# Group norm in the trips of the RWKV scan, the first norm joined to the parameter block, key tile 0 among the low-rank products

## What is computed

```python
u = rms_norm(h, norm1_g[i])
xs = h[:, :, None, :] + (prev - h)[:, :, None, :] * mu        # h here is u, prev is u one token earlier
rkv = jnp.einsum('btjd,jde->btje', xs[:, :, :3], w_in)         # r, k, v
decay, a, gate = ...                                           # low-rank products: w1 w2, a1 a2, g1 g2
def step(S, inp):                                              # S: 64 x 64 for each head
    sa = jnp.einsum('bhvk,bhk->bhv', S, -kk_t)
    S = S * w_t[:, :, None, :] + sa[..., None] * (kk_t * a_t)[:, :, None, :] + v_t[..., None] * k_t[:, :, None, :]
    return S, jnp.einsum('bhvk,bhk->bhv', S, r_t)
mean = jnp.mean(y, axis=-1, keepdims=True)                     # group norm: over the 64 of each head
var = jnp.mean(jnp.square(y - mean), axis=-1, keepdims=True)
y = (y - mean) * lax.rsqrt(var + RW_GN_EPS) * ln_w + ln_b
y = y + jnp.sum(r_h * k_h * r_k, axis=-1, keepdims=True) * v_h # the bonus
y = y.reshape(B, T, D) * gate
h = h + y @ w_out
```

## Time and profile before

| | us |
|---|---|
| median of 3 runs | 3041.53 (3041.08 to 3042.39) |
| the profiled execution | 3047.19 |
| its span, first to last instruction | 3045.4 |
| TensorE busy | 2654.7 (87%) |
| VectorE busy | 884.6 (29%) |
| ScalarE busy | 548.9 (18%) |
| GpSimd busy | 218.2 (7%) |

### The profile page before, as it was taken

One profiled execution on the slowest core, in us unless ns is written; L12 is line 12 of the kernel. 1 busy time (PEld: TensorE's weight loads), 2 busy tenths in 40 slices (PEclk: granted clock), 3 DMA queues, 4 the chain that ended last, 5 costly groups with the idle time before them and its releaser, 6 DMA issues. The chain is left out here.

```text
span 3045.4 us, 44485 instructions
## 1 busy us (share of the span) xinstructions
PE 2654.7 (87%) x18608; PEld 1421.0 (47%) x18608; DVE 884.6 (29%) x1598; ACT 548.9 (18%) x892; POOL 218.2 (7%) x209
## 2 busy tenths in 40 slices
PE   5798996989887695999999969999669869999993
PEld 2243442888885253444443434444544534444441
DVE  6233001666565534111110122000762431101013
ACT  3342000223233311000000011300451100000000
POOL 0000000001010400001010000000010010100100
PEclk9999998999998897999999989999889979999997
DMA  3242133131323523799999940221433259999995
GB/s 117 112 143 99 62 103 97 45 82 48 82 49 151 212 118 140 259 413 410 411 407 399 392 152 38 94 79 55 118 130 136 95 196 377 417 413 417 413 404 225
DMA packets 264767, 617.51 MB, mean 203 GB/s; under 512 B 37377, under 2 KB 128658, under 8 KB 262546
## 3 DMA queue, kind: packets, MB, share of 16 engines
q1 hardware_dynamic: 233362, 524.72, 46.3%
q10 hardware_dynamic: 17408, 56.63, 4.7%
q0 software_dynamic: 13824, 33.58, 2.8%
HBM read 545.67 MB, written 85.98 MB: 207 GB/s over the span
## 5 line engine op out<-in xcount | busy, mean ns | idle before, releaser
L1812 PE MATMUL moe_first_psum<-moe_ring,moe_first_x_t 128*64 128x512 f32 (+1 forms) x1504 | 508.9, 599 | 7.3 <-DMA moe_ring<-in_moe_w_in 3.7
L560 PE MATMUL proj_psum<-proj_mix,proj_ring 128*128 128x512 f32 x768 | 337.1, 599 | 15.9 <-ACTq L72 10.1
L1812 PEld LDWEIGHTS moe_first_psum<-moe_ring,moe_first_x_t 128*64 128x64 f32 (+1 forms) x1504 | 198.1, 165 | 280.0 <-issue 275.2
L1812 PE MATMUL moe_first_psum<-moe_ring,moe_first_act_t 128*128 128x512 f32 (+1 forms) x800 | 282.1, 594 | 0.0
L1408 PE MATMUL moe_route_psum<-moe_ring,trunk_mixed 128*128 128x512 f32 x512 | 230.3, 605 | 22.8 <-PEq L106 22.8
L560 PEld LDWEIGHTS proj_psum<-proj_mix,proj_ring 128*128 128x128 f32 x768 | 147.1, 193 | 200.4 <-issue 188.7
L1853 DVE TENSOR_TENSOR moe_first_act<-moe_first_silu,moe_first_psum 128x512 f32<-128x512 f32 x48 | 33.0, 688 | 688.6 <-ACT moe_first_silu L1869 688.6
L2146 PE MATMUL hproj_psum<-trunk_mixed,moe_ring 128*128 128x512 f32 x512 | 220.0, 592 | 1.8 <-ACTq L72 1.8
L1812 PE MATMUL moe_first_psum<-trunk_mixed,moe_first_x_t 128*128 128x512 f32 (+1 forms) x544 | 196.1, 593 | 0.0
L1812 PEld LDWEIGHTS moe_first_psum<-moe_ring,moe_first_act_t 128*128 128x128 f32 (+1 forms) x800 | 105.8, 162 | 131.5 <-issue 131.5
L1408 PEld LDWEIGHTS moe_route_psum<-moe_ring,trunk_mixed 128*128 128x128 f32 x512 | 96.9, 194 | 137.2 <-issue 137.2
(11 more groups left out here) (339 smaller groups left out, 3075.2 us busy)
## 6 DMA issues: line engine op xcount, KB each, us to landing
moe_ring<-in_moe_w_in SPq DMA_DIRECT2D x94, 2048.0 KB, 18.0
moe_ring<-in_moe_w_out SPq DMA_DIRECT2D x50, 2048.0 KB, 19.9
trunk_mixed<-in_moe_w_in SPq DMA_DIRECT2D x34, 2048.0 KB, 20.3
trunk_mixed<-in_moe_w_out SPq DMA_DIRECT2D x14, 2048.0 KB, 21.1
moe_ring<-expert_rows SPq DMA_DIRECT2D x16, 1024.0 KB, 7.9
proj_ring<-in_rw_in SPq DMA_DIRECT2D x12, 1024.0 KB, 6.1
moe_ring<-gate_cm SPq DMA_DIRECT2D x16, 512.0 KB, 4.4
normed_rows<-moe_x SPq DMA_DIRECT2D x16, 512.0 KB, 2.6
```

Source lines behind the costliest of these rows:

```text
L560: mm = pe.matmul(psum[:, bank + half, :], ring[slot][:, k, part * P:(part + 1) * P], src[:, k, half * HALF:(half + 1) * HALF], start=(k == ...
L1812: mm = t.matmul(e.psum[rows, bank + a, :], left[:, k0 + k, rows], weights.units[m % RING][:, k, a * HALF:(a + 1) * HALF], start=(part != " ...
```

## The change

Four edits:

1. The block `norm` is gone. `setup` now holds its work: SyncE first loads two groups of x, then the parameters, then the other two groups, then all low-rank weights. VectorE, after each tile's gain, also makes that tile's part of `delta`; the single operation over all of it is gone.
2. In `rwkv_project` the weights of key tile 0 (`first_w`, 512 KB) are loaded into a buffer of their own, and its products are issued by TensorE among the up products: after each of the eight pairs, two of the sixteen multiplies of 512 columns. The ring's first slot is loaded after the second down product, no longer after the last up product.
3. The group norm moves into the scan. The mean is taken out of v in the projection already: for each v tile VectorE sums over heads and subtracts, where it copied before. In trip n of the scan tile n - 1 (128 tokens, all channels) is normed: square, logarithm and exponential on ScalarE, sums over heads on TensorE, scaling on GpSimd, eight operations of scale and shift on ScalarE, then the bonus and the gate on GpSimd. The bonus of tile n is summed on TensorE in trip n from r times k, which GpSimd multiplies. v and gate are loaded once more for each trip, 512 KB each. The out-projection's weights are loaded at the scan's start. All five lists are written out over the trips.
4. The block `rwkv_output` is gone; the norm of the last tile of tokens stands at the head of `out_route`. The rooms for weights are split in two, so that part of them is free for the group norm during the scan; the load of unit 5 waits until the last tile is done.

The core of the diff:

```diff
 def setup(nc, io, c, front):
         def _(sp):
+            for q in range(2):
+                front.load_x(sp, q)
...
+            for q in range(2, TT // 2):
+                front.load_x(sp, q)
+            front.load_lora(sp)
...
         def _(v):
+                    v.tensor_tensor(u[:, :, 1 + at:1 + at + P], ..., spread(gain, 2, P), ALU.mult).then_inc(dve.sem, 1)
+                    v.wait_ge(dve.sem, dve.after("gain", tile))
+                    v.tensor_sub(delta[:, :, at:at + P], u[:, :, at:at + P], u[:, :, 1 + at:1 + at + P])
 def rwkv_project(nc, io, c, front, d):
+            sp.dma_start(first_w, weights[0][:, :, 0:P]).then_inc(first_in, 16)
+                    if n == 0:
+                        sp.wait_ge(lora_h, 2)
+                    if n == 1:
+                        sp.wait_ge(lora_tiles, 3 * KT)
...
-            v.tensor_sub(delta[:], u[:, :, 0:T], u[:, :, 1:T + 1]).then_inc(mixed, 1)
...
+                    v.tensor_reduce(head_total[:], rows_p, AX_X, ALU.add).then_inc(v_dve.sem, 1)
-                    v.tensor_copy(mix[0][:, b, :], psum[:, 4 + 2 * b:6 + 2 * b, :].rearrange("p a t -> p (a t)")
+                    v.scalar_tensor_tensor(out=mix[0][:, b, :].rearrange("p (n e) -> p n e", e=HEAD),
+                                           in0=spread(head_total[:], 2, HEAD), scalar=-1.0 / HEAD, in1=rows_p,
+                                           op0=ALU.mult, op1=ALU.add).then_inc(v_dve.sem, 1)
...
+            def first_keys(n):
+                half, k = n // KT, n % KT
...
+                return pe.matmul(psum[:, half, :], first_w[:, k, :], mix[1][:, k, half * HALF:(half + 1) * HALF],
+                                 start=(k == 0), stop=(k == KT - 1))
             for tile in range(KT):
...
                 mm.then_inc(lora_tiles, 2)
+                for n in range(2):
+                    mm = first_keys(2 * tile + n)
+            mm.then_inc(k_pe.sem, 1)
...
-            for tile in range(KT):
+            for tile in range(1, KT):
+class GroupNorm:
+    def square(self, a, y, g):
+        return a.activation(self.inverse, y[:, :, g * P:(g + 1) * P], ACT.Square)
+    def sums(self, t, c, source, banks):
+        for half in range(NH):
+            mm = t.matmul(banks[half].rearrange("p (m t) -> p m t", t=P), c.head_ones[:],
+                          source[:, half * (PAIRS // 2):(half + 1) * (PAIRS // 2), :], start=True, stop=True)
+    def bonus_sums(self, t, weights, source, banks):
+        for m in range(PAIRS):
+            mm = t.matmul(at, weights[:, m, :], source[:, m, :], start=True, stop=True)
+    def log(self, a, c, banks, half):
+        return a.activation(..., ACT.Ln, scale=1.0 / HEAD, bias=c.gn_eps[:])
+    def root(self, a):
+        return a.activation(self.inverse, self.inverse, ACT.Exp, scale=-0.5)
+    def unit(self, g, y, tile):
+        for at, pairs in self.pieces(y, tile):
+            ins = g.tensor_tensor(at, at, self.inverse[:, pairs, :], ALU.mult)
+    def affine(self, a, c, y, tile, done):
+        for m in range(PAIRS):
+            a.activation(at, at, ACT.Identity, scale=..., bias=...).then_inc(done, 1)
+    def finish(self, g, y, tile, added, finished):
+        for n, (at, pairs) in enumerate(self.pieces(y, tile)):
+            g.tensor_tensor(at, at, self.bonus[:, pairs, :], ALU.add).then_inc(added, 1)
...
+            ins = g.tensor_tensor(at, at, self.gate[:, pairs, :], ALU.mult)
 def rwkv_scan(nc, c, d, y, gn, outw):
         def _(sp):
+            load_tile("v", 0, gn.value, value_in)
+            load_tile("gate", 0, gn.gate, gate_in)
+            outw.load(sp)
         def _(g):
             def body(trip, last):
                 decayed(trip, 1)
+                bonus_terms(trip)
+                if trip:
+                    g.wait_ge(rooted, trip)
+                    gn.unit(g, y, trip - 1).then_inc(united, 1)
+                    g.wait_ge(shifted, PAIRS * trip)
+                    g.wait_ge(bonus_made, 2 * trip)
+                    g.wait_ge(gate_in, 16 * trip)
+                    gn.finish(g, y, trip - 1, bonus_added, finished)
         def _(v):
+                        if j == 3 and b == 1:
+                            bonus(trip)
         def _(a):
+            a.preload_act_table_set("natural_log_exp_and_others")
+                    if b == 0 and trip:
+                        gn.square(a, y, trip - 1).then_inc(squared, 1)
+                    if b == 1 and trip:
+                        a.wait_ge(united, trip)
+                        gn.affine(a, c, y, trip - 1, shifted)
...
+                        if b == 0 and trip and j == 2:
+                            a.wait_ge(summed, trip)
+                            for h in range(2):
+                                gn.log(a, c, sum_banks, h).then_inc(logged, 1)
+                        if b == 0 and trip and j == 3:
+                            gn.root(a).then_inc(rooted, 1)
         def _(t):
+                        if j == 1 and b == 0 and trip:
+                            gn.sums(t, c, gn.inverse, sum_banks).then_inc(summed, 1)
+                        if j == 1 and b == 1:
+                            gn.bonus_sums(t, rk_ones, rk, sum_banks).then_inc(bonus_summed, 1)
-def rwkv_output(nc, io, c, d, y, weights, room):
 def out_route(..., gn=None):
+            if gn is not None:
+                t.wait_ge(gn_squared, 1)
+                gn.sums(t, c, gn.inverse, gn_banks).then_inc(gn_summed, 1)
```

531 lines of the change are left out of this document (260 added, 271 removed).

## The result

The changed kernel takes 2971.38 us (median of 4 runs, 2968.3 to 2975.17) where the kernel before takes 3041.96: ratio 0.9766, 95% interval 0.9749 to 0.9782. That is 70.6 us less; 64.1 less had been forecast, for 2977.4. The profiled execution of before is 5.2 above its median, which is why the traces lie further apart than the medians.

What follows compares the result with a forecast made beforehand. The norm stage was taken as bound by a chain through four engines, the scan's levels by TensorE. Terms -7.2 - 17 - 85.8 + 1.3 + 44.6 = -64.1 from 3041.5 gave 2977.4 us, range 2950 to 3012.

Steps and rivals of the forecast that it cites:

- Front, -7.2: Start of the kernel: earlier x and `delta` made in pieces bring the first blend from 45.4 to 38.2; bounds 4 and 10.
- Key tile 0, -17: Low-rank up products: tile 0's products mostly fill TensorE's idle time, a pair every 3.55 us; saves 17, bounds 7 and 18.
- Group norm's stage, -85.8: Stage after the scan: its 88.60 us go, 2.8 return at the out-projection's head; net 85.8, bounds 83 and 88.
- The v tile's 1.3: Projection of layer 0's v: only the last tile's head reduction shows, 1.3 us lost (1.1 to 1.5).
- Scan, +44.6: Scan: grows by 21.6 (b = 0), 18.9 (b = 1), 2.1 (last chunk) and 2 (trip 0); bounds 22 and 84.
- the second case: Rival on the scan: it pays for TensorE's list alone, 22 us, giving 2955; chance 20%.
- two meetings of VectorE and GpSimd: Scan, b = 0 chunks: r times k stretches L890 by about 0.7, scaling by the root stretches L871 by 0.62.
- the bonus products on VectorE: Scan, b = 1 chunks, level 3: two products of 512 elements, 0.68 each, less one wait of 0.59: 0.8 us.
- two more loads: Scan, b = 1 chunks: loading v and gate again, 1 MB, costs 0.8 us a trip (0 to 3).
- The third: Rival on the scan: upper bounds paid, 84 us, through new meetings and loads starving instruction fetch, giving 3017; chance 14%.
- the fourth: Rival on key tile 0: it is not hidden, little but reordering, and saves 7 us, giving 2987; chance 7%.
- the fifth: Rival, slower: GpSimd's 16 pieces a trip hold up VectorE, TensorE's work unhidden, 3 a trip for fetch: 3055; chance 4%.

Runs made afterwards that it cites:

- front_apart: Changed kernel with x loaded behind the parameters again and `delta` made by one operation, the block still joined: 2978.73 us.
- before_shifted: Kernel before plus one unused constant of 4 bytes a partition, which moves every later tile by 32 bytes: 3052.25 us.
- aligned: Changed kernel with two unused spacers, so that the experts' weight regions and the scan's loaded tiles start at multiples of 256 bytes: 2950.35 us.
- fresh_spaced: Changed kernel with the scan's five 512 KB loads for the next trip issued in three groups instead of at once: 2953.86 us.
- gpsimd_left_out: Changed kernel without twelve of GpSimd's sixteen new pieces a trip (inverse root, bonus, gate; r times k stays): 2973.2 us.

## Why the prediction was right or wrong, step by step

**Front, -7.2.** Right in size and near in its reasons: the first blend stood at 38.23. The reciprocal was forecast at 12.0 and came at 12.93. The parameters, forecast at 8.7, had TensorE's transposition at 10.86, near the bound of 11.1, and so VectorE's columns and the mean behind them came 0.73 after ScalarE was ready. By the rows of front_apart, 3.6 are from x first, 2.2 from the joined block and 1.4 from the pieces of `delta`. 1.6 of the 7.2 were lost by the up products; over the first 14.6 us from the first blend TensorE's granted clock was 0.75, where it had been 0.84.

**Key tile 0, -17.** Measured 17.7 (23.3 less 5.6). The pace was mis-sized: 3.83 a pair where I had 3.55. My own terms give 3.75 (3.20 + 1.76 - 1.21), so 3.55 was an error of the sum, and the four passes took 1.92 where I had 1.76. The higher clock of the first two pairs made up for it: from the first up product to tile 1 passed 31.55, and the forecast had 31.5. The working had no separate term for the wait of 5.76 that went; the run with the products moved back showed that it carries more than the interleaving.

**Group norm's stage, -85.8.** Measured 86.6. The sums ran at a granted clock of 0.53, 3.34 for 1.76, and the products behind them gained 2.6, which I had counted as nothing. The rest of the last tile cost nothing, as forecast. The v tile's 1.3 is there: from the first operation on the last v tile to its store pass 2.64, where it was 1.40. But the gain at the scan's start is 23.3 after 23.4 at key tile 1, so the projections between were as much shorter, for a reason that I haven't traced.

**Scan, +44.6.** This step failed. It grew by 22.8 in this pair of traces, the lower end of the bounds, which the second case named. Per chunk: b = 0 +2.13 for 3.1, b = 1 +0.96 for 2.7, the last +2.19 for 2.1, trip 0's first chunk -1.0 for +2. The terms for TensorE were near: 1.98 for the sums (1.76 forecast) and 2.05 for the bonus sums (2.13), half of the latter covered by the wait in the level where VectorE sums the decays, as forecast (1.1 net). What failed are the terms of the other engines: 1.3 a trip for two meetings of VectorE and GpSimd, 0.8 for the bonus products on VectorE, 0.8 for two more loads. Neither meeting came where it was forecast: the products with the rise (L871 before, L985 after) take 0.9 in the seven places where they took 1.3, and L1004 is stretched by the pieces for bonus and gate (L777, L780), not by r times k, which stretches the copy of the ends by 0.4. The run without twelve of the pieces shows that those for bonus and gate are covered. The other two terms have no run of their own; a b = 1 chunk grew by 0.96, less than the 1.1 forecast for the bonus sums alone, so nothing of them shows. I had added to the path what I had seen lengthen on an engine that waits 0.59 in each half level; the row that showed VectorE waiting for TensorE was in my hands and spoke against it. If the written-out lists gave back some 5 in this scan, up to 5 us of such terms could be hidden behind it.

**What the sum lacked, +11.9.** The experts. The prediction has no word on the split of the ring or on the new constant, since neither changes the number or the bytes of a load. They change its place, and the experts run at the limit of DMA and TensorE at once (shares of 1.02 and 1.00 in the windows above), where 401 GB/s for 410 is seen. Without this the changed kernel would have come out near 2960 (2971.4 - 11.9), 18 below the forecast. The miss in the scan (22 too dear) and this one hid each other, so that the total came so near is luck.

**Rivals.** The second, the scan at +22, was right on the scan. The third is refuted by the scan's growth, the fourth by key tile 0's 17.7, the fifth by the measured time itself and by the run without twelve of GpSimd's sixteen pieces, which shows no price for them. The third and the fifth also charge a starved instruction fetch, the fifth with 3 us a trip; no run shows that term, only waits without a releaser, in the stretch of the scan 21.3 us in all before and 17.1 after.

## What to carry to other kernels

Ask of each term of a sum on which engine's list it lies, and add those of other engines only where a row shows the bounding engine waiting for them: here the scan grew by about what TensorE's list got (33 us more of work, 9 us less of waits), while VectorE, ScalarE and GpSimd were busy 142 us more beside it; for twelve of GpSimd's sixteen pieces a run shows no cost that can be measured. When an edit adds a constant or splits a buffer, look where all later tiles start: an unused constant of 4 bytes ahead of the experts' weight ring cost 12 us. Where one of two equal chunks is longer, look for a burst of loads beside it before looking at its work: spacing the burst gave 17.5 us, moving half of the bonus sums nothing.

## What the runs showed of the hardware

The place of the tiles changes how fast the experts' weights land. With one unused constant of 4 bytes ahead of them, 2 MB take 22.6 us from issue to landing in the ring and 18.0 without it (before_shifted and before, same code), and the page's slices of layer 0's experts read 409, 408, 404 and 400 GB/s for 413, 410, 411 and 407. With spacers of 128 bytes ahead of `mixed` and `late` and 96 more ahead of `early`, they take 17.9, 17.8 and 19.4 us in `early`, `late` and the units in `mixed`, and 21.1, 23.1 and 23.5 without them (aligned and after, same code). Each edit moved all of these tiles at once; which of them costs most, and which places are fast beyond the ones run, is open.

TensorE without any releaser, called issue, beside a burst of 2.5 MB of loads: 17 us in one scan (after), 6 when the same bytes come in three groups (fresh_spaced). It varies by several us from one profile to the next: 22.0 in before, 15.5 in before_shifted, the same code. So a difference of 5 us there needs the runs' medians and not two traces.

Some of VectorE's operations take longer beside GpSimd's: L1004, which has two inputs in SBUF, takes 0.68 to 0.70 in all 30 instances of the scan without the pieces for root, bonus and gate (gpsimd_left_out), and 1.10 to 1.16 in ten of those with them (after; 0.84 on average). No price in the time could be measured. The copy of the ends has one input and is stretched too, 0.59 for the 0.18 of before; in after one copy ends at 566.73 and GpSimd's piece beside it at 566.70.
